# One step of Strassen in the first MLP product: seven block products, weight sums on GpSimd, last norm block by block

## The chip, the core and the metric

The kernel runs on one core of one Trainium2 chip. The metric is the device time in microseconds (us) of one execution, as the median of several. Five engines work side by side: TensorE (PE in the profile, with its weight loads as PEld), VectorE (DVE), ScalarE (ACT), GpSimd (POOL) and SyncE (SP), which issues the transfers. They wait for one another through semaphores.

## What is computed

A network of two blocks over 1024 tokens of width 1024 (an attention and convolution block of two layers, then a mixer block), and at its end an MLP and a norm. The change touches only this end:

```python
h = rms_norm(x, norm_mlp)                      # 1024 tokens x 1024
u = jnp.square(jax.nn.relu(h @ w_up))          # 1024 x 4096
x = x + u @ w_down                             # back to 1024 x 1024
return rms_norm(x, norm_final)
```

All is float32. The kernel keeps that accuracy on a bfloat16 array: each operand is split into a high part (rounded to bfloat16) and a low part (the rest), and each product is three matmuls (`mm3`: high x high, low x high, high x low).

## The kernel before

**Weights.** All weights come as 130 chunks of 128 x 2048 float32 (1 MB), in one order, `CHUNKS`. SyncE loads chunk n into one of two places of `stage` once chunk n-2 has been split. GpSimd (the loop from L504) splits it: four casts of 128x512 to `w_hi` (L513), four subtractions of 128x512 to `w_lo` (L520). `w_hi` and `w_lo` hold four chunks, so the split of chunk n waits until TensorE has used chunk n-4.

**MLP.** The 4096 hidden channels are taken in 16 rounds of 256. Chunk `up{j}` is the 1024 x 256 piece of the up weights of round j, `dn{j}` the 256 x 1024 piece of the down weights. TensorE's order is `MLP`: up0, up1, dn0, up2, dn1, ... up15, dn14, dn15. An up chunk is 96 matmuls of 128x512 (`gemm_f`: two groups n of 128 channels, two halves of the tokens, eight steps of k, three matmuls each). A down chunk is 96 too (eight token tiles t, 12 matmuls for each half). `ht_hi`, `ht_lo` (hT) hold the normed input, transposed: 128 x 8 x 1024.

**After an up chunk.** For each n: ScalarE evacuates PSUM with relu into RT[n] (`evac`, L1361), VectorE squares RT[n] (`squared`, L2104), ScalarE casts it into the high part of RS (L1477), VectorE subtracts for the low part (`square_lo`, L2108). RS holds two rounds. After a down tile VectorE adds it into the residual XR (`add_down`, L2116). VectorE's order is by hand: in round j the square of up j+1 comes ahead of the eight adds of dn j.

**PSUM.** There are eight banks of 128x512 float32: `big0`, `big1` (two banks each) and `bank[0..3]`. A tile of 1024 columns takes two. The pool "mlp" turns through four such tiles: big0, big1, banks 0 and 1, banks 2 and 3. `take` makes TensorE wait for whoever last read the banks it takes.

**Beginning of the MLP.** up0 runs inside `first_gemm(3, ...)` (L604) while the last parts of hT are written by `ht_half`; its two results lie in big1 (n = 0) and big0 (n = 1). up1 takes big0 first, so it waits for the evacuation of up0, n = 1.

**End.** ScalarE computes the sum of squares of each token tile as soon as its last add is done (L1484, L1486). SyncE loads the gain NF after the last matmul, and then VectorE makes the eight output tiles (L2139 reciprocal, L2142 multiply), through two buffers FO that go out by transfers of 512 KB (L494).

## Time and profile before

| | |
|---|---|
| time, median of 3 runs (range) | 3247.94 us (3245.13 to 3251.59) |
| profiled execution: its time / its span | 3242.97 us / 3241.1 us |
| TensorE busy | 3021.7 us, 93% of the span |
| VectorE, ScalarE, GpSimd busy | 55%, 33%, 29% |
| mean granted TensorE clock | 0.967 of full |
| matmuls of the 16 MLP rounds | from about 2553 us to 3217.7 us of the span |

The profile is of one execution. Its page lists busy time by engine and by group of instructions (line, engine, operation, tiles, shapes). The trace behind it can be asked for stretches of time, for waits (which engine waited for which instruction), and for instructions in order of time. A matmul is shown with a duration of 0.38 us, but matmuls are pipelined: what counts is the distance from one start to the next.

### The profile page before, as it was taken

Reading aid. Unit: us, or ns where it says so; the run is one execution under the profiler, and the core shown is the slowest. Engines: PE = TensorE matmul, PEld = TensorE weight load, DVE = VectorE, ACT = ScalarE, POOL = GpSimd, SP = SyncE. Lnnn points to the kernel's source line nnn. Section 1 sums busy time; section 2 is a strip of 40 time slices with the busy share of each in tenths; the row PEclk is TensorE's granted clock in tenths of the full one; section 3 lists DMA queues with packets and bytes.
Section 4 is the critical chain, followed back from the end, with each engine's and each line's share of the span. In section 5 each row is a group of like instructions: output and inputs, shape, how many; then the busy total and the mean of one; then the engine's idle time right before and its main releaser. Section 6 shows DMA issues by size and latency. Waiting matters only on the chain.

```text
span 3241.1 us, 48311 instructions
## 1 busy us (share of the span) xinstructions
PE 3021.7 (93%) x19783; PEld 1875.1 (58%) x20010; DVE 1767.4 (55%) x2951; ACT 1070.0 (33%) x1880; POOL 948.3 (29%) x958
## 2 busy tenths in 40 slices
PE   7979997999979978989999999999999999999997
PEld 7439875884439658854555655655654444444443
DVE  2575796773589976645265364365363333333334
ACT  2353544662356636633122132222122211001111
POOL 2301364000603470004323223323221433333320
PEclk9997998999999989999999999999899999999998
DMA  7313231002201321022111111111112111111101
GB/s 242 135 59 121 74 129 66 15 21 98 88 14 67 127 95 31 25 85 85 52 40 39 40 40 40 39 40 40 40 40 78 65 52 52 52 48 46 51 27 59
DMA packets 49164, 207.13 MB, mean 64 GB/s; under 512 B 4488, under 2 KB 9776, under 8 KB 32304
## 3 DMA queue, kind: packets, MB, share of 16 engines
q1 hardware_dynamic: 42288, 195.63, 17.2%
q10 hardware_dynamic: 6656, 8.39, 0.8%
q8 instruction: 159, 2.61, 0.3%
q14 instruction: 61, 0.50, 0.0%
HBM read 187.22 MB, written 16.79 MB: 63 GB/s over the span
## 4 chain that ended last, share of the span: by engine, by line
PE 79%; DVE 14%; issue 3%; ACT 3%; DMA 1%; POOL 1%; SPq 0%; DVEq 0%; ACTq 0%; POOLq 0%
PE big L268 18%; PE big L269 18%; PE big L267 18%; PE banks L267 4%; PE banks L268 4%; PE banks L269 4%; PE banks L1015 3%; DVE arena L1686 2%; PE banks L874 1%; DVE arena L1911 1%; PE big L550 1%; PE banks L550 1%; DVE arena L2075 1%; DVE arena L1891 1%; DVE arena L2020 1%
## 5 line engine op out<-in xcount | busy, mean ns | idle before, releaser
L513 POOL CAST w_hi<-stage 128x512 bf16<-128x512 f32 x432 | 282.2, 695 | 1796.4 <-PE big L269 1427.6
L520 POOL TENSOR_TENSOR w_lo<-stage,w_hi 128x512 bf16<-128x512 f32 x520 | 670.4, 1320 | 397.3 <-ACT w_hi L1187 396.6
L268 PE MATMUL big<-ht_lo,w_hi 128*128 128x512 bf16 x1412 | 536.7, 380 | 4.8 <-DVE ht_lo L1584 1.8
L267 PE MATMUL big<-ht_hi,w_hi 128*128 128x512 bf16 x1388 | 527.3, 380 | 13.0 <-DVE arena L1938 6.5
L269 PE MATMUL big<-ht_hi,w_lo 128*128 128x512 bf16 x1414 | 537.2, 380 | 1.5
L267 PE MATMUL big<-w_hi,ht_hi 128*128 128x256 bf16 (+1 forms) x1272 | 381.3, 300 | 18.1 <-POOL w_lo L520 9.2
L268 PE MATMUL big<-w_lo,ht_hi 128*128 128x256 bf16 (+1 forms) x1274 | 382.2, 300 | 4.0 <-issue 3.7
L269 PE MATMUL big<-w_hi,ht_lo 128*128 128x256 bf16 (+1 forms) x1276 | 382.3, 300 | 0.3
L267 PEld LDWEIGHTS big<-ht_hi,w_hi 128*128 128x128 bf16 x1440 | 143.1, 99 | 180.8 <-issue 14.9
L269 PEld LDWEIGHTS big<-ht_hi,w_lo 128*128 128x128 bf16 x1440 | 141.2, 98 | 171.0 <-issue 1.9
L268 PEld LDWEIGHTS big<-ht_lo,w_hi 128*128 128x128 bf16 x1440 | 141.3, 98 | 163.5 <-issue 4.4
L1361 ACT ACTIVATE arena<-big 128x1024 f32<-128x1024 f32 x66 | 67.5, 1023 | 429.0 <-PE big L269 428.8
L1699 DVE TENSOR_SCALAR_CACHE_REDUCE arena<-arena,smalli 128x512 bf16<-128x512 f32 (+5 forms) x268 | 206.7, 827 | 2.4
L267 PEld LDWEIGHTS big<-w_hi,ht_hi 128*128 128x128 bf16 x1280 | 151.0, 118 | 62.3 <-issue 10.8
L267 PE MATMUL banks<-w_hi,arena 128*128 128x128 bf16 (+2 forms) x696 | 174.7, 273 | 8.3 <-POOL w_lo L520 6.3
L268 PE MATMUL banks<-w_lo,arena 128*128 128x128 bf16 (+2 forms) x700 | 176.2, 274 | 0.4
L269 PE MATMUL banks<-w_hi,arena 128*128 128x128 bf16 (+2 forms) x698 | 175.6, 274 | 0.2
L269 PEld LDWEIGHTS big<-w_hi,ht_lo 128*128 128x128 bf16 x1280 | 150.4, 117 | 39.2 <-issue 1.7
L1263 ACT ACTIVATE arena<-arena,smalli 128x896 bf16<-128x896 f32 x124 | 134.8, 1088 | 115.0 <-DVE smalli L1845 115.0
L268 PEld LDWEIGHTS big<-w_lo,ht_hi 128*128 128x128 bf16 x1280 | 150.3, 117 | 38.1 <-issue 1.1
L1015 PE MATMUL banks<-arena 128*128 128x64 f32 x896 | 120.9, 291 | 29.7 <-DVE arena L2029 23.4
L1015 PEld LDWEIGHTS banks<-arena 128*128 128x128 f32 x896 | 115.7, 207 | 55.5 <-DVE arena L2029 43.0
(325 smaller groups left out, 5947.1 us busy)
## 6 DMA issues: line engine op xcount, KB each, us to landing
stage<-in_w SPq DMA_DIRECT2D x130, 1024.0 KB, 4.8
arena<-in_w_ada SPq DMA_DIRECT2D x48, 512.0 KB, 4.2
arena<-in_x SPq DMA_DIRECT2D x16, 512.0 KB, 7.5
xs<-arena SPq DMA_DIRECT2D x16, 512.0 KB, 2.6
arena<-xs SPq DMA_DIRECT2D x16, 512.0 KB, 7.8
gt<-arena ACTq DMA_DIRECT2D x16, 256.0 KB, 2.5
arena<-gt ACTq DMA_DIRECT2D x16, 256.0 KB, 2.6
out_x<-arena SPq DMA_DIRECT2D x8, 512.0 KB, 2.6
```

The lines of the kernel that those rows point to most:

```text
L267: pe.matmul(out, ah, bh, start=start, stop=False)
L268: pe.matmul(out, ah, bl, start=False, stop=False)
L269: return pe.matmul(out, al, bh, start=False, stop=stop)
L513: pool.tensor_copy(w_hi[:, n % RING, c0:c1], stage[:, n % RAW_RING, c0:c1]).then_inc(s_w_hi_split, mark(s_w_hi_split, n, q))
L520: ins = pool.tensor_tensor(w_lo[:, n % RING, c0:c1], stage[:, n % RAW_RING, c0:c1], w_hi[:, n % RING, c0:c1], ALU.subtract)
L550: ins = pe.matmul(g[:, (n * 4 + q) * 8 + k:(n * 4 + q) * 8 + k + 1], ada_buf(i)[:, k % 2, q * P:(q + 1) * P], s_(S_C + k), start=True, sto ...
L874: ins = pe.transpose(g[:, (s - q0) * P:(s - q0 + 1) * P], PB[h % 2][:, s * P:(s + 1) * P], ident)
L1015: ins = pe.matmul(g[:, s * 64:(s + 1) * 64].rearrange("p (j h) -> p j h", h=h), KF[c][:, s * P:(s + 1) * P], q, start=True, stop=True)
L1263: ins = act.activation(is_over[tb], score[tb], ACT.Sign, scale=-1.0, bias=smalli[:, 8 + j:9 + j].bitcast(F32), accum_out=s_(S_CNT + j))
L1361: act.activation(out, tile(pool, *key)[:, :], func, **kw).then_inc(s_read_act, mark(s_read_act, *key))
L1686: dve.scalar_tensor_tensor(score[tb], PB[i % 2][:, 0:N], w, score[tb], ALU.mult, ALU.add).then_inc(s_acc, mark(s_acc, l, i))
L1699: ins = dve.tensor_scalar(is_over[tb], score[tb], thr(j), 0.0, op, ALU.add, accum_out=cnt[:, j:j + 1])
```

## The change

The pieces `up2` to `up15` (the constant `STRASSEN`) are computed by one step of Strassen's scheme, in Winograd's form. The weight piece is seen as 2 x 2 blocks of 512 x 128, hT as 2 x 2 blocks of 512 x 512. Seven products of such blocks take the place of eight; `seven_products` issues them, in the order p1, p2, p6, p5, p7, p3, p4, each into one bank of 128x512 of the new pool "st" (`bank[0..3]`, in turn, the turn going on from round to round).

- GpSimd makes, per up chunk, four sums of weight blocks (128x512, float32), then seven casts and seven subtractions for the parts of the seven weight operands, in place of four and four. The parts are laid in the chunk's place and in `SUMX`, which has two places. The first of these chunks, up2, waits until hT is complete.
- The four sums of hT blocks (`TT`, high and low parts) are made once, in two halves g, by VectorE and ScalarE together (`token_sums`): 14 operations of 128x1024 on VectorE and 4 on ScalarE for each half. The first half stands ahead of the evacuation of up0 on ScalarE and ahead of its square on VectorE, the second behind the last `square_lo` of up0.
- For a seven-product round ScalarE copies p1 from PSUM; VectorE joins the rest by seven additions of 128x512 with one input from PSUM (`quarters`), straight into RT. There is no relu on ScalarE: `squared` is now max with 0 and multiply in one instruction.
- At the end NF is loaded after the last up product (NF, FO and the ScalarE junk tile lie where `TT` was), and VectorE makes output tile t-1 right behind the add of tile t (`finish`).
- The host lays out the up weights of these rounds by block.

The core of the diff:

```diff
+STRASSEN = range(2, 16)
...
+        pools = {"big": two[0:2], "t": one[0:2], "o": one[2:4], "c": one[0:3], "f": one[3:4], "c2": two[2:4], "mlp": two, "st": one}
...
-            sp.wait_ge(s_gemm, when(s_gemm, "dn", 15, NT - 1))
+            sp.wait_ge(s_gemm, when(s_gemm, "st", 15, "p4"))
             sp.dma_start(NF, AP_["norm_final"].partition_broadcast(P)).then_inc(s_nf_in, mark(s_nf_in, by=16))
...
+                if CHUNKS[n][1].startswith("up") and int(CHUNKS[n][1][2:]) in STRASSEN:
+                    j = int(CHUNKS[n][1][2:])
+                    a11, a12, a22, a21 = [stage[:, n % RAW_RING, 512 * i:512 * (i + 1)] for i in range(4)]
+                    s1, s2, s3, s4 = SUMF
+                    if j == STRASSEN[0]:
+                        pool.wait_ge(s_ht_lo, when(s_ht_lo, "all", 3))
+                    else:
+                        pool.wait_ge(s_w_split, when(s_w_split, n - 2))
+                    pool.tensor_tensor(s1, a21, a22, ALU.add).then_inc(s_sum, mark(s_sum, j, 3))
+                    pool.tensor_tensor(s3, a11, a21, ALU.subtract).then_inc(s_sum, mark(s_sum, j, 5))
+                    pool.wait_ge(s_sum, when(s_sum, j, 3))
+                    pool.tensor_tensor(s2, s1, a11, ALU.subtract).then_inc(s_sum, mark(s_sum, j, 4))
+                    pool.wait_ge(s_sum, when(s_sum, j, 4))
+                    pool.tensor_tensor(s4, a12, s2, ALU.subtract).then_inc(s_sum, mark(s_sum, j, 6))
+                    parts = ((0, a11), (1, a12), (2, a22), (3, s1), (5, s3), (4, s2), (6, s4))
+                    for i, x in parts:
+                        if i > 2:
+                            pool.wait_ge(s_sum, when(s_sum, j, i))
+                        pool.tensor_copy(sum_part(j, i)[0], x).then_inc(s_sum_hi, mark(s_sum_hi, j, i))
+                    for i, x in parts:
+                        pool.wait_ge(s_sum_hi, when(s_sum_hi, j, i))
+                        hi, lo = sum_part(j, i)
+                        ins = pool.tensor_tensor(lo, x, hi, ALU.subtract)
+                    ins.then_inc(s_w_split, mark(s_w_split, n))
+                    continue
...
+            def seven_products(j):
+                b11, b21, b22 = [x[:, 0:4, 0:512] for x in hT], [x[:, 4:8, 0:512] for x in hT], [x[:, 4:8, 512:1024] for x in hT]
+                for name, i, b in (("p1", 0, b11), ("p2", 1, b21), ("p6", 4, TT[1]), ("p5", 3, TT[0]), ("p7", 5, TT[2]), ("p3", 6, b22), ("p4", 2, TT[3])):
+                    if j == STRASSEN[0] and name == "p6":
+                        pe.wait_ge(s_t_lo, when(s_t_lo, 1, 3))
+                    w = [x.rearrange("p (k n) -> p k n", k=4) for x in sum_part(j, i)]
+                    g = take(pe, "st", "st", j, name)
+                    for k in range(4):
+                        ins = mm3(pe, g, [x[:, k, :] for x in w], [x[:, k, :] for x in b], k == 0, k == 3)
+                    ins.then_inc(s_gemm, mark(s_gemm, "st", j, name))
+                chunk_used(2, f"up{j}", s_gemm)
             for c, j in MLP[1:]:
                 pe.wait_ge(s_w_split, when(s_w_split, CHUNK_AT[(2, f"{c}{j}")]))
-                if c == "up":
+                if c == "up" and j in STRASSEN:
+                    seven_products(j)
+                elif c == "up":
                     gemm_f(2, f"up{j}", 0, ("up", j, 0), pool="mlp")
                     gemm_f(2, f"up{j}", 1, ("up", j, 1), pool="mlp")
...
+            def token_sums(g):
+                for i in range(4):
+                    act.wait_ge(s_t_sum, when(s_t_sum, g, i))
+                    act.activation(TT[i][0][:, 2 * g:2 * g + 2, :], TS[(0, 1, 2, 0)[i]], ACT.Copy).then_inc(s_t_hi, mark(s_t_hi, g, i))
+            def square_hi(j, n):
+                if j >= 2:
+                    act.wait_ge(s_gemm, when(s_gemm, "dn", j - 2, NT - 1))
+                act.wait_ge(s_r2, when(s_r2, j, n))
+                act.activation(RS[j % 2][0][:, n, :], RT[n], ACT.Copy).then_inc(s_rs_hi, mark(s_rs_hi, j, n))
             for c, j in MLP:
-                if c == "up":
+                if c == "up" and j in STRASSEN:
+                    if j > STRASSEN[0]:
+                        act.wait_ge(s_c_out, when(s_c_out, j - 1, "u2"))
+                    act.wait_ge(s_gemm, when(s_gemm, "st", j, "p1"))
+                    act.activation(PU[0], tile("st", "st", j, "p1"), ACT.Copy).then_inc(s_p_out, mark(s_p_out, j))
+                    freed(s_p_out, "st", j, "p1")
+                    square_hi(j, 0)
+                    square_hi(j, 1)
+                elif c == "up":
+                    token_sums(j)
                     for n in range(2):
                         if j:
                             act.wait_ge(s_rs_lo, when(s_rs_lo, j - 1, n))
                         evac(RT[n], ACT.Relu, "up", j, n, pool="mlp" if j else "big")
-                        if j >= 2:
-                            act.wait_ge(s_gemm, when(s_gemm, "dn", j - 2, NT - 1))
-                        act.wait_ge(s_r2, when(s_r2, j, n))
-                        act.activation(RS[j % 2][0][:, n, :], RT[n], ACT.Copy).then_inc(s_rs_hi, mark(s_rs_hi, j, n))
+                        square_hi(j, n)
...
+            def token_sums(g):
+                near, far = slice(2 * g, 2 * g + 2), slice(4 + 2 * g, 6 + 2 * g)
+                b11, b12 = [[x[:, near, 512 * t:512 * (t + 1)] for x in hT] for t in range(2)]
+                b21, b22 = [[x[:, far, 512 * t:512 * (t + 1)] for x in hT] for t in range(2)]
+                def low(i):
+                    dve.wait_ge(s_t_hi, when(s_t_hi, g, i))
+                    dve.tensor_tensor(TT[i][1][:, near, :], TS[(0, 1, 2, 0)[i]], TT[i][0][:, near, :], ALU.subtract).then_inc(s_t_lo, mark(s_t_lo, g, i))
+                t1, t2, t3 = TS
+                step(dve.tensor_tensor(t1, b12[0], b11[0], ALU.subtract))
+                step(dve.tensor_tensor(t1, t1, b12[1], ALU.add))
+                dve.tensor_tensor(t1, t1, b11[1], ALU.subtract).then_inc(s_t_sum, mark(s_t_sum, g, 0))
+                dve.wait_ge(s_t_sum, when(s_t_sum, g, 0))
+                step(dve.tensor_tensor(t2, b22[0], t1, ALU.subtract))
+                dve.tensor_tensor(t2, t2, b22[1], ALU.add).then_inc(s_t_sum, mark(s_t_sum, g, 1))
+                step(dve.tensor_tensor(t3, b22[0], b12[0], ALU.subtract))
+                step(dve.tensor_tensor(t3, t3, b22[1], ALU.add))
+                dve.tensor_tensor(t3, t3, b12[1], ALU.subtract).then_inc(s_t_sum, mark(s_t_sum, g, 2))
+                low(0)
+                dve.wait_ge(s_t_lo, when(s_t_lo, g, 0))
+                dve.wait_ge(s_t_sum, when(s_t_sum, g, 1))
+                step(dve.tensor_tensor(t1, b21[0], t2, ALU.subtract))
+                dve.tensor_tensor(t1, t1, b21[1], ALU.add).then_inc(s_t_sum, mark(s_t_sum, g, 3))
+                low(1)
+                low(2)
+                low(3)
+                dve.wait_ge(s_t_lo, when(s_t_lo, g, 3))
+            def quarters(j):
+                def add(name, out, x, p, *after):
+                    dve.wait_ge(s_gemm, when(s_gemm, "st", j, p))
+                    for a in after:
+                        dve.wait_ge(s_c_out, when(s_c_out, j, a))
+                    dve.tensor_tensor(out, x, tile("st", "st", j, p), ALU.add).then_inc(s_c_out, mark(s_c_out, j, name))
+                c11, c12, c21, c22 = RT[0][:, 0:512], RT[0][:, 512:1024], RT[1][:, 0:512], RT[1][:, 512:1024]
+                dve.wait_ge(s_rs_lo, when(s_rs_lo, j - 1, 1))
+                dve.wait_ge(s_p_out, when(s_p_out, j))
+                add("c11", c11, PU[0], "p2")
+                freed(s_c_out, "st", j, "p2")
+                add("u2", PU[1], PU[0], "p6")
+                freed(s_c_out, "st", j, "p6")
+                add("t", c12, PU[1], "p5", "u2")
+                freed(s_c_out, "st", j, "p5")
+                add("u3", c21, PU[1], "p7")
+                add("c22", c22, c12, "p7", "t")
+                freed(s_c_out, "st", j, "p7")
+                add("c12", c12, c12, "p3", "c22")
+                freed(s_c_out, "st", j, "p3")
+                add("c21", c21, c21, "p4", "u3")
+                freed(s_c_out, "st", j, "p4")
             def squared(j, n):
-                dve.wait_ge(s_read_act, when(s_read_act, "up", j, n))
-                dve.tensor_tensor(RT[n], RT[n], RT[n], ALU.mult).then_inc(s_r2, mark(s_r2, j, n))
+                if j in STRASSEN:
+                    dve.wait_ge(s_c_out, when(s_c_out, j, "c21" if n else "c12"))
+                else:
+                    dve.wait_ge(s_read_act, when(s_read_act, "up", j, n))
+                dve.scalar_tensor_tensor(RT[n], RT[n], 0.0, RT[n], ALU.max, ALU.mult).then_inc(s_r2, mark(s_r2, j, n))
...
+            token_sums(0)
+            squared(0, 0)
+            square_lo(0, 0, 0, T)
+            squared(0, 1)
+            square_lo(0, 1, 0, T)
+            token_sums(1)
+            for j in range(16):
+                if j + 1 in STRASSEN:
+                    quarters(j + 1)
+                if j < 15:
+                    squared(j + 1, 0)
+                    square_lo(j + 1, 0, 0, T)
+                for t in range(NT):
+                    add_down(j, t)
+                    if j == 15 and t:
+                        finish(t - 1)
+                    if j < 15 and t == 0:
+                        squared(j + 1, 1)
+                    if j < 15 and t == 2:
+                        square_lo(j + 1, 1, 0, 512)
+                    if j < 15 and t == 3:
+                        square_lo(j + 1, 1, 512, T)
+            finish(NT - 1)
```

## Rows read from the trace of the kernel before

**Rows 1.** Stretch of the MLP rounds: length, busy (count) by engine, PEclk, DMA share, GB/s.

```profile
2600.00:3213.00 613.00, 610.00 (x2785) 277.88 (x2840) 230.40 (x198) 66.50 (x72) 192.13 (x211) 1.00 0.12 43
```

**Rows 2.** Waits of PE, 2566:2700: who waited for whom, us, times, longest.

```profile
PE big L267 <- ACT arena L1361: 1.2, 1, 1.2
```

**Rows 3.** VectorE in order of time (start, us, what, [idle, releaser]), two rounds' first squares.

```profile
2628.38 1.23 DVE L2104 TENSOR_TENSOR arena<-arena 128x1024 f32<-128x1024 f32 x1 [10.25 <-ACT arena L1361]
...
2669.82 1.22 DVE L2104 TENSOR_TENSOR arena<-arena 128x1024 f32<-128x1024 f32 x1 [10.26 <-ACT arena L1361]
```

**Rows 4.** Groups by shape, 2500:3241: count, busy us, mean ns, idle before.

```profile
L520 POOL TENSOR_TENSOR w_lo<-stage,w_hi 128x512 bf16<-128x512 f32 x128 | 159.6, 1277 | 0.0
...
L2116 DVE TENSOR_TENSOR arena<-arena,big 128x1024 f32<-128x1024 f32 x64 | 78.1, 1220 | 113.9 <-PE big L269 113.9
...
L2142 DVE SCALAR_TENSOR_TENSOR arena<-arena,small 128x1024 f32<-128x1024 f32 x8 | 10.3, 1285 | 4.4 <-DMA out_x<-arena 3.9 <-DVE small L2139 0.4
```

**Rows 5.** Line L1719: min/median/max ns, first and last start, shape.

```profile
L1719 DVE TENSOR_TENSOR arena<-banks,arena x16: 679/686/692, 347.6 to 1082.9; 128x512 bf16<-128x512 f32 x16
```

**Rows 6.** In order of time: a PSUM tile handed from PE to DVE and back.

```profile
2547.79 0.38 PE L269 MATMUL big<-w_hi,arena 128*128 128x512 bf16 x1
...
2548.20 1.22 DVE L2095 TENSOR_TENSOR arena<-arena,big 128x1024 f32<-128x1024 f32 x1 [8.28 <-PE big L269]
...
2549.68 0.38 PE L267 MATMUL big<-ht_hi,w_hi 128*128 128x512 bf16 x1 [1.52 <-DVE arena L2095]
```

**Rows 7.** In order of time: DVE, ACT and PE around the end of up0.

```profile
2563.67 2.76 DVE L1540 SCALAR_TENSOR_TENSOR ht_lo<-banks,small,ht_hi 128x512 bf16<-128x512 f32 x4 [4.11 <-ACT ht_hi L1079]
...
2571.23 1.06 ACT L1477 ACTIVATE arena<-arena 128x1024 bf16<-128x1024 f32 x1 [1.29 <-DVE arena L2104]
2574.09 1.02 ACT L1361 ACTIVATE arena<-big 128x1024 f32<-128x1024 f32 x1 [1.81 <-PE big L269]
...
2575.26 0.38 PE L267 MATMUL big<-ht_hi,w_hi 128*128 128x512 bf16 x1 [1.21 <-ACT arena L1361]
```

**Rows 8.** The chain that ended last: start us, us, two dependent VectorE steps.

```profile
2471.00 1.24 DVE arena L2083
2472.27 1.24 DVE arena L2084
```

**Rows 9.** POOL in order of time: a split alone, then one beside VectorE.

```profile
2561.48 2.28 POOL L513 CAST w_hi<-stage 128x512 bf16<-128x512 f32 x4
2563.72 4.49 POOL L520 TENSOR_TENSOR w_lo<-stage,w_hi 128x512 bf16<-128x512 f32 x4
2574.19 3.27 POOL L513 CAST w_hi<-stage 128x512 bf16<-128x512 f32 x4 [5.98 <-PE big L269]
...
146.21 7.43 POOL L520 TENSOR_TENSOR w_lo<-stage,w_hi 128x512 bf16<-128x512 f32 x4
```

**Rows 10.** VectorE in order of time, beside the last two rows of Rows 9.

```profile
2575.15 1.28 DVE L2104 TENSOR_TENSOR arena<-arena 128x1024 f32<-128x1024 f32 x1 [1.61 <-ACT arena L1361]
...
147.25 4.27 DVE L1647 TENSOR_TENSOR arena<-arena 128x1024 bf16<-128x1024 f32 x2
```

**Rows 11.** PE in order of time after an idle stretch, then a window as in Rows 1.

```profile
234.39 0.43 PE L267 MATMUL big<-w_hi,ht_hi 128*128 128x256 bf16 x1 [4.66 <-DVE arena L1517]
...
238.88 0.32 PE L267 MATMUL big<-w_hi,ht_hi 128*128 128x256 bf16 x1
...
236.00:238.00 2.00, 2.00 (x11) 1.56 (x10) 2.00 (x5) 0.00 (x0) 0.00 (x0) 0.50 0.00 0
```

**Rows 12.** In order of time: the last add, the last sum of squares, output, last multiply.

```profile
3217.78 1.22 DVE L2116 TENSOR_TENSOR arena<-arena,big 128x1024 f32<-128x1024 f32 x1 [1.37 <-PE big L269]
...
3220.22 0.29 ACT L1486 ACTIVATE small<-small 128x1 f32<-128x1 f32 x1
...
3223.64 14.25 SPq L494 DMA_DIRECT2D out_x<-arena  x8
...
3236.25 1.28 DVE L2142 SCALAR_TENSOR_TENSOR arena<-arena,small 128x1024 f32<-128x1024 f32 x1 [0.38 <-DVE small L2139]
```

More of the change, by code:

```diff
@@ L1483, in _ @@
                     act.wait_ge(s_sq, when(s_sq, "m", 3, NT - 1))
[L1484 removed]
+                act.activation(JNK_END, XR[:, i, :], ACT.Square, accum_out=s_(S_SSQ + i)).then_inc(s_sq, mark(s_sq, "f", 4, i))
                 act.wait_ge(s_sq, when(s_sq, "f", 4, i))
@@ L2110, in square_lo, with finish @@
                     ins.then_inc(s_rs_lo, mark(s_rs_lo, j, n))
[L2112 to L2135 removed]
+            def finish(i):
                 dve.wait_ge(s_rms, when(s_rms, "f", 4, i))
@@ L2214, in pack_2 @@
     for j in range(16):
-        put(2, f"up{j}", f["w_up_2"][0][:, j * 256:(j + 1) * 256])
+        up = f["w_up_2"][0][:, j * 256:(j + 1) * 256]
+        if j in STRASSEN:
+            for i, (n, k) in enumerate(((0, 0), (0, 1), (1, 1), (1, 0))):
+                part = up[k * 512:(k + 1) * 512, n * P:(n + 1) * P].reshape(4, P, P).transpose(1, 0, 2)
+                w[CHUNK_AT[(2, f"up{j}")]][:, i * 512:(i + 1) * 512] = part.reshape(P, 512)
+        else:
+            put(2, f"up{j}", up)
         put(2, f"dn{j}", f["w_down_2"][0][j * 256:(j + 1) * 256, :])
```

51 lines of the change are left out of this document (23 added, 28 removed).

## The prediction

> **What bounds the kernel now.** I first read the windows by engine, for the stretch in which the MLP rounds run undisturbed. The reader is to see TensorE busy 610.0 of 613.0 us at a granted clock of 1.00, GpSimd busy 192 us, VectorE 230 us [rows 1]. Then the waits of TensorE: between 2566 and 2700 us of the span there is one, 1.2 us, and it lies ahead of up1 [rows 2]; asked for 2590 to 3213 us, the same view lists none. So these rounds are bound by the number of matmuls alone, and the other engines lie beside them. One round lasts from one first square to the next, 2669.82 - 2628.38 = 41.44 us [rows 3], for 192 matmuls: 0.2158 us each. Two places of the MLP are not bound so: its beginning, where ScalarE and VectorE stand between up0 and up1 [rows 7], and its end, where 23.4 us of the span come after the last matmul (it ends just before the last add starts, at 3217.78) [rows 12].
>
> **Fewer matmuls.** Seven products of 12 matmuls are 84 in place of 96. 14 rounds x 12 x 0.2158 = 36.3 us less on TensorE, all of it on the path. Weight loads stay one for each matmul. The round becomes 41.44 - 2.59 = 38.85 us.
>
> **GpSimd.** A cast costs 2.28/4 = 0.57 us, a subtraction of 128x512 4.49/4 = 1.12 us when nobody disturbs it [rows 9]; the four sums have two float32 inputs and a float32 output, which no row shows; the nearest is that subtraction, and I take 1.12 (between 0.57, the one-input row, and 1.86, the disturbed subtraction of rows 9). A pair of chunks costs 4 x 1.12 + 7 x 0.57 + 7 x 1.12 + (2.28 + 4.49) = 23.1 us of 38.85. The split of up j may begin when up j-2 is used and is needed two down chunks and one up chunk later, 59.6 us. It is hidden even if it doubles. The transfers of chunks wait for splits two back, and are hidden with them.
>
> **VectorE in a round.** The seven joins have one input from PSUM; the nearest row is 0.69 us for 128x512 [rows 5]. Per round: 8 adds x 1.22, 7 joins x 0.69, two squares now at 1.28 (the three-operand form) and two low parts at 1.23 [rows 3, 4]: 19.6 us of 38.85. The joins follow the products (2.59 us each) one by one and end with p4. What is new is the order: the first square now waits for the last product. Counted from the end of p4: join 0.8, square 1.3, ScalarE's cast 1.2, low part 1.3, first add 1.2: 5.8 us; with squares and low part slowed by GpSimd (below) 7.8. The fifth down tile, which takes the first one's banks, starts at 10.4. Hidden, with 2.6 us to spare.
>
> **The handover of p4's bank.** This is not hidden. The pool "st" goes on turning, so p4 lies in bank (6 - (j - 2)) mod 4: for j = 3, 4, 7, 8, 11, 12, 15 this is bank 0 or 1, which the first down tile takes. There TensorE must wait until VectorE has read p4. The same handover with an operation of 1.22 us put the next matmul 1.67 us behind its place (2547.79 + 0.22 to 2549.68) [rows 6], so 0.45 plus the operation: 0.69 + 0.45 = 1.14 us, 7 times: 8.0 us. In the other seven rounds p4 lies in bank 2 or 3, and the second down tile comes 2.59 us later: nothing. Bounds: 0 and 14 x 1.14 = 16.
>
> **Token sums at the beginning.** TensorE ends up0 just before 2574.09, and up1 can start when ScalarE has evacuated up0, n = 1: at 2575.26 now [rows 7]. In the changed order ScalarE does that after its cast of the first square, which comes after the first square, which comes after all 14 VectorE operations of the first token sums. These begin when hT is complete, 2563.67 + 2.76 = 2566.4. Dependent steps follow at 1.27 us [rows 8], independent ones at about 1.14: 17.4 us undisturbed. But GpSimd starts up2's sums at that very moment, since it waits for the same event. How the two slow one another: where GpSimd subtracts, two VectorE operations with two SBUF inputs took 4.27 us (clean 2.46), and GpSimd's four took 7.43 (clean 4.49) [rows 9, 10]: VectorE goes at 0.57 of its pace, GpSimd at about 0.44. Where GpSimd casts, VectorE took 1.28 for 1.23, and GpSimd lost 0.99 us beside it: 0.96 and 0.23. So: GpSimd's four sums last 4.49/0.44 = 10.2 us, in which VectorE does 5.8 of its 17.4 us; the other 11.6 run beside casts in 12.1. The sums end at 2588.7. Then square 1.3, cast 1.1, evacuation 1.0, handovers 0.3: up1 starts at about 2592.4, **17.1 us later** than now. TensorE has then idled 18 us, and its clock falls: after 4.66 us of idleness it ran at half (a granted 0.50) from 234.39 to 238.88 us [rows 11], which lost 2.2 us; I take 2.2.
>
> The second token sums come after the remaining squares and low parts of up0 (about 2598) and run beside GpSimd's subtractions of up2, then its casts and subtractions of dn1: by the same rates about 23.7 us, to 2621.6. The evacuation of up1, n = 1, whose banks the fourth tile of dn0 takes, waits behind them and a square, a cast and itself: 2626. The fourth tile could start at 2592.4 + 20.7 + 2.2 + 3 x 2.59 = 2623.1: 3.0 us lost. The beginning costs 17.1 + 2.2 + 3.0 = 22.3 us. If nothing slowed anything: sums to 2583.8, up1 at 2587.6, 12.3 + 2.2 = 14.5 us.
>
> The Trainium skill, GPSIMD Engine Reference, Key points, says that GpSimd's SBUF interfaces contend with VectorE instructions that have two SBUF inputs, and makes no exception for casts. The rows above show next to no slowing of VectorE beside casts, and I go by them; what the rule gives taken literally is rival 2 below.
>
> **The end.** Now: last matmul 3217.7, last add 3217.78 to 3219.0, last sum of squares and root to 3220.51, last multiply to 3237.53, span to 3241.1 [rows 12]. After: the gain is there, seven tiles are out already, and behind 3220.51 come 0.2 of reciprocal, one multiply of 1.28 [rows 4] and the same 3.6 us of output: 3225.6. **15.5 us less.** Within dn15 VectorE has an add, a reciprocal and a multiply per tile, about 2.55 us against TensorE's 2.59: just hidden, with four tiles of PSUM as a cushion.
>
> **Sum.** 36.3 + 15.5 - 8.0 - 22.3 = 21.5 us less. The profiled execution of before took 3242.97 us (span 3241.1): 3221.5 by it. The median of the runs shown is 5 us higher, 3247.94, and the same difference gives **3226.5**, my forecast for the median.
>
> **Rivals**, all against the median:
> 1. *The sums aren't slowed.* Reading bfloat16 or the four-byte sums could leave GpSimd's and VectorE's accesses apart. For: operations with a PSUM input keep 1.22 throughout [rows 4]. Against: rows 9 and 10. Beginning 14.5: 3218.7.
> 2. *Every one of the 28 token operations is slowed*, at 2.17 us, whatever GpSimd does. Then the first sums end at 2597.4, up1 starts at 2601.8 (26.5 late), the second sums end at about 2639 and dn0 waits 10.9, each with a clock loss of 2.2: 41.8 us. 36.3 + 15.5 - 8.0 - 41.8 = 2.0: 3246. Against: the row beside casts.
> 3. *GpSimd becomes the bound*, the case on the other side. Its pair of chunks adds time from 38.85 us on, and the kernel becomes slower than before by 0.2% where the pair passes 41.4 us (28 us lost, and the 8.0 of p4 hidden, over 14 rounds). With all 15 two-input operations at 7.43/4 = 1.86 us and half of the 11 casts stretched to 0.57/0.23 = 2.5 us a pair takes 27.9 + 13.7 + 3.1 = 44.7: 5.9 us a round over, x 14 = 83 us, while the waits for p4 (8.0) vanish in it: 3301. Against: it needs VectorE on two SBUF inputs almost all the time, and it is so for 5.0 us a round.
> 4. *Joins later than the products.* Every round waits at the first down tile, and for two joins, not one: 14 x (0.45 + 1.38) = 25.6 in place of 8.0: 3244. For: the joins are a chain with waits of VectorE on itself. Against: half its time is free.
> 5. *The products don't come at 0.2158 us a matmul*: seven groups of 12 with a look at a semaphore each in place of two of 48. Each group 0.1 us later is 9.8 us: 3236. The down tiles of before have one for every 24 matmuls, and [rows 1, 3] leave no room for a gap.
>
> **How the numbers follow.** Forecast case 0.60 (3219 to 3235, the spread of the slowing and of the p4 wait), rival 1 0.14, rival 2 0.09, rival 3 0.03, rival 4 0.06, rival 5 0.08. The range 3214 to 3241 holds the forecast case, rivals 1 and 5 and part of 4; it leaves out 2, 3 and the rest. A measurement of this kernel can tell 0.2%, 6.5 us, from no change: faster means under 3241.4. Faster: 0.60 + 0.14 + 0.08 + 0.02 + 0.02 (the early parts of 2 and 4) = 0.86; same 0.10; slower 0.04.
>
> **What would show it.** Matmuls 168 fewer, and rounds of about 38.9 and 40.0 us. In the waits of TensorE: seven waits of about 1 us on the last join, one of about 18 us on ScalarE's evacuation ahead of up1, and a few us in dn0. The clock at half for some us behind up1's start. Token operations of 1.2 to 2.2 us, by what GpSimd does. About 8 us between the last matmul and the end of the span. A wait of TensorE on w_lo in the rounds would show rival 3. The prediction is wrong if the beginning costs more than 40 us, or if each round waits.

## The result and the profile after

| | before | after |
|---|---|---|
| median (range, executions) | 3248.19 us (3245.13 to 3251.59, 4) | 3230.86 us (3228.2 to 3234.91, 4) |
| span of the profiled execution | 3241.1 us | 3226.4 us |
| first stretch: to hT complete | 2566.4 us | 2570.9 us |
| second stretch: from hT complete to the end | 674.7 us | 655.5 us |

The ratio after/before is 0.9947 (95% interval 0.9933 to 0.9961, so 13 to 22 us less): 17.3 us less by the medians, where 21.5 had been forecast. The last two rows cut each span where hT is complete, which is where the change begins to act (the last `ht_lo` operation on VectorE: 2563.67 + 2.76 before [rows 7], 2568.16 + 2.76 after). The first stretch holds the same instructions in both kernels. It came out between 2563.9 and 2573.3 us in the twelve profiles of this study, whatever the kernel, with the granted clock of TensorE in it 0.96 or 0.97. So single spans differ by up to 9 us for reasons outside the MLP, and below I compare second stretches: 19.2 us less.

The page's busy times after, then TensorE's waits from 2566 us to the end of the span (us in total, times, longest):

```profile
PE 2994.1 (93%) x19618; PEld 1864.1 (58%) x19842; DVE 1908.7 (59%) x3077; ACT 1058.3 (33%) x1874; POOL 1151.7 (36%) x1098
...
PE big L275 <- ACT arena L1418: 23.7, 2, 21.6
PE banks L275 <- DVE arena L2212: 6.4, 7, 1.0
```

Where before stood one wait of 1.2 us [rows 2] there are now nine: two on ScalarE's evacuation, seven on VectorE's last join (L2212 is the addition of `quarters`). The view shows nothing on the weight parts.

The beginning, in order of time (start us, us, engine and line); first VectorE with the token sums, GpSimd beside it, then ScalarE and TensorE, and windows as in [rows 1]:

```profile
2572.09 2.17 DVE L2188 TENSOR_TENSOR arena<-arena,ht_lo 128x1024 f32<-128x1024 f32 x1
...
2584.01 1.51 DVE L2195 TENSOR_TENSOR arena<-arena,ht_lo 128x1024 f32<-128x1024 f32 x1
...
2590.09 5.81 DVE L2184 TENSOR_TENSOR arena<-arena 128x1024 bf16<-128x1024 f32 x3
...
2595.94 2.06 DVE L2236 SCALAR_TENSOR_TENSOR arena<-arena 128x1024 f32<-128x1024 f32 x1
...
2573.14 2.25 POOL L536 TENSOR_TENSOR arena<-stage 128x512 f32<-128x512 f32 x1
...
2579.75 4.71 POOL L545 CAST w_hi<-stage 128x512 bf16<-128x512 f32 x3
...
2590.61 6.30 POOL L549 TENSOR_TENSOR w_lo<-stage,w_hi 128x512 bf16<-128x512 f32 x3
...
2598.99 1.01 ACT L1418 ACTIVATE arena<-big 128x1024 f32<-128x1024 f32 x1
...
2600.14 0.59 PE L275 MATMUL big<-ht_hi,w_hi 128*128 128x512 bf16 x1 [21.59 <-ACT arena L1418]
...
2602.00:2604.00 2.00, 2.00 (x7) 0.67 (x5) 1.29 (x1) 0.67 (x1) 2.00 (x2) 0.50 0.00 0
2604.00:2606.00 2.00, 2.00 (x7) 0.78 (x6) 1.58 (x2) 0.38 (x1) 2.00 (x3) 0.57 0.51 66
2606.00:2608.00 2.00, 2.00 (x11) 0.89 (x10) 1.97 (x2) 0.00 (x0) 2.00 (x3) 1.00 0.90 377
```

A token operation took 2.17 us beside GpSimd's two-input operations and 1.51 beside its casts; a cast beside it 4.71/3 = 1.57. The seven casts were done by about 2590.6, so the last three of the token operations met subtractions again: 5.81/3 = 1.94 us each. The first 14 ran from 2570.8 to 2595.9. TensorE idled 21.6 us, and its clock stood at half when it came back, until about 2605.7.

Two handovers of p4's bank, in TensorE's order of time, and the start of two up splits (GpSimd), one round apart:

```profile
2900.87 0.38 PE L277 MATMUL banks<-arena,w_lo 128*128 128x512 bf16 x1
2902.23 0.38 PE L275 MATMUL banks<-w_hi,arena 128*128 128x512 bf16 x1 [0.98 <-DVE arena L2212]
...
2743.81 1.26 POOL L535 TENSOR_TENSOR arena<-stage 128x512 f32<-128x512 f32 x1 [11.39 <-issue]
...
2783.80 1.27 POOL L535 TENSOR_TENSOR arena<-stage 128x512 f32<-128x512 f32 x1 [11.39 <-issue]
```

The next matmul comes 1.36 us after the last, not 0.22: 1.14 us lost. A round with a handover has 39.99 us, where 38.85 are the matmuls. GpSimd idles 11.4 us of it.

The end, to hold against [rows 12]: the last add, the last multiply, and the transfers of the output as SyncE issued them:

```profile
3219.03 1.22 DVE L2257 TENSOR_TENSOR arena<-arena,big 128x1024 f32<-128x1024 f32 x1
...
3221.99 1.28 DVE L2251 SCALAR_TENSOR_TENSOR arena<-arena,small 128x1024 f32<-128x1024 f32 x1
...
3206.13 17.51 SPq L511 DMA_DIRECT2D out_x<-arena  x8
```

From the start of the last add to the end of the span: 7.4 us, where it was 23.3.

### The profile page after: what moved, and what is told of

Same layout as the page of the kernel before. It is cut to its first block, busy times and chain, and to the rows that moved or that the text cites. A ratio compares the mean times of both kernels' runs of the same rounds, so it can differ in the third digit from the quotient of the medians.

```text
span 3226.4 us, 48326 instructions
## 1 busy us (share of the span) xinstructions
PE 2994.1 (93%) x19618; PEld 1864.1 (58%) x19842; DVE 1908.7 (59%) x3077; ACT 1058.3 (33%) x1874; POOL 1151.7 (36%) x1098
## 4 chain that ended last, share of the span: by engine, by line
PE 76%; DVE 16%; issue 3%; ACT 3%; POOL 1%; DMA 0%; SPq 0%; DVEq 0%; ACTq 0%; POOLq 0%
PE big L276 16%; PE big L277 16%; PE big L275 16%; PE banks L275 5%; PE banks L277 5%; PE banks L276 5%; PE banks L1057 4%; DVE arena L1760 2%; PE banks L916 2%; DVE arena L1985 1%; PE big L592 1%; PE banks L592 1%; DVE arena L2149 1%; DVE arena L1965 1%; DVE arena L2094 1%
## 5 line engine op out<-in xcount | busy, mean ns | idle before, releaser
L555 POOL CAST w_hi<-stage 128x512 bf16<-128x512 f32 x376 | 252.3, 713 | 1449.9 <-PE big L277 1241.1
L562 POOL TENSOR_TENSOR w_lo<-stage,w_hi 128x512 bf16<-128x512 f32 x464 | 600.6, 1326 | 396.8 <-ACT w_hi L1244 396.2
L275 PE MATMUL big<-ht_hi,w_hi 128*128 128x512 bf16 x1168 | 444.9, 381 | 33.4 <-ACT arena L1418 21.6
L276 PE MATMUL big<-ht_lo,w_hi 128*128 128x512 bf16 x1193 | 454.4, 381 | 4.5 <-DVE ht_lo L1658 1.8
L277 PE MATMUL big<-ht_hi,w_lo 128*128 128x512 bf16 x1194 | 454.4, 381 | 1.2
L275 PEld LDWEIGHTS big<-ht_hi,w_hi 128*128 128x128 bf16 x1216 | 121.2, 100 | 175.7 <-issue 36.1
L277 PEld LDWEIGHTS big<-ht_hi,w_lo 128*128 128x128 bf16 x1216 | 119.4, 98 | 145.1 <-issue 2.8
L276 PEld LDWEIGHTS big<-ht_lo,w_hi 128*128 128x128 bf16 x1216 | 119.3, 98 | 137.4 <-issue 4.9
L2212 DVE TENSOR_TENSOR arena<-arena,banks 128x512 f32<-128x512 f32 x98 | 66.2, 687 | 180.2 <-PE banks L277 180.2
L2094 DVE COPY_PREDICATED arena<-con,banks 128x512 f32<-128x512 int32 x56 | 58.8, 1049 | 164.7 <-PE banks L1057 164.5
L1057 PE MATMUL banks<-arena 128*128 128x64 f32 x896 | 124.7, 297 | 30.1 <-DVE arena L2103 23.7
```

The source lines that it names most:

```text
L275: pe.matmul(out, ah, bh, start=start, stop=False)
L276: pe.matmul(out, ah, bl, start=False, stop=False)
L277: return pe.matmul(out, al, bh, start=False, stop=stop)
L555: pool.tensor_copy(w_hi[:, n % RING, c0:c1], stage[:, n % RAW_RING, c0:c1]).then_inc(s_w_hi_split, mark(s_w_hi_split, n, q))
L562: ins = pool.tensor_tensor(w_lo[:, n % RING, c0:c1], stage[:, n % RAW_RING, c0:c1], w_hi[:, n % RING, c0:c1], ALU.subtract)
L1057: ins = pe.matmul(g[:, s * 64:(s + 1) * 64].rearrange("p (j h) -> p j h", h=h), KF[c][:, s * P:(s + 1) * P], q, start=True, stop=True)
```

## The experiments

My theory after this: the prediction's parts are right, and the beginning is dearer than forecast, since VectorE is slowed beside casts too. Rivals: the token operations are slow in themselves; the p4 waits are a symptom of something else; GpSimd paces the rounds after all. Second stretches of all kernels (hT complete to the end of the span, one profiled execution each), with the ratio of the executions' times to those of the kernel before. The intervals of after, e1_bank and e2_quiet overlap, so what those two edits are worth is read from the second stretch and the trace:

| kernel | second stretch, us | ratio (95% interval) | TensorE's waits in it, us |
|---|---|---|---|
| before | 674.7 | 1 | 1.2 |
| after | 655.5 | 0.9947 (0.9933 to 0.9961) | 23.7 evacuation, 6.4 joins |
| e1_bank | 652.0 | 0.9929 (0.9915 to 0.9944) | 26.5 evacuation |
| e2_quiet | 650.1 | 0.9937 (0.9925 to 0.9949) | 17.1 evacuation, 6.4 joins |
| e3_end | 659.3 | 0.9966 (0.9954 to 0.9978) | 1.2 |
| e4_order | 665.6 | 0.9973 (0.9962 to 0.9985) | 32.5 evacuation, 6.5 joins |
| e5_best | 626.9 | 0.9852 (0.9829 to 0.9875) | 2.9 evacuation |
| e6_sums2 | 662.6 | 0.9967 (0.9955 to 0.9978) | 29.2 evacuation, 6.4 joins |
| e7_parts2 | 668.0 | 0.9984 (0.9971 to 0.9996) | 25.8 evacuation, 6.5 joins, 6.7 adds |
| e8_same | 655.5 | one execution | 23.9 evacuation, 6.4 joins |
| e9_parts3 | 807.1 | one execution | 25.5 evacuation, 6.4 joins, 119.0 weight parts |
| e10_products | 673.9 | 0.9989 (0.9977 to 1.0) | 26.5 evacuation, 6.4 joins |

### e1_bank: the bank turn anew in every round

```diff
+                turns["st"] = 0
                 for name, i, b in (("p1", 0, b11), ("p2", 1, b21), ("p6", 4, TT[1]), ("p5", 3, TT[0]), ("p7", 5, TT[2]), ("p3", 6, b22), ("p4", 2, TT[3])):
```

> The changed kernel with one edit: the bank turn of the seven products starts anew in every round, so that the last product always lies in bank 2 and the first down tile never takes its bank. Theory (the seven waits of TensorE on the last join, 6.4 us by the view of waits plus the restarts, are what is left of the seven-product rounds' loss): 7 to 8 us less than the changed kernel, about 3223 us, no wait of TensorE on a join line, every seven-product round 38.85 us. Rival (the first down tile is late for another reason, such as VectorE's order, and the wait only moves to another releaser): the same time as the changed kernel, 3231 us, with as many waits on another line.

Its view of waits has no join, and its up splits start exactly 38.85 us apart (2747.75, 2786.60):

```profile
2747.75 1.27 POOL L535 TENSOR_TENSOR arena<-stage 128x512 f32<-128x512 f32 x1 [11.38 <-issue]
...
2786.60 1.27 POOL L535 TENSOR_TENSOR arena<-stage 128x512 f32<-128x512 f32 x1 [11.38 <-issue]
```

So the seven waits were the handover and nothing else. The total fell by less, 3.5 us of second stretch, because of the beginning: TensorE's restart in dn0 came 35.0 us behind up1's first matmul in place of 33.6 (1.4 us), and behind this longer wait, 4.9 us in place of 2.1, the clock stood at half for some 5.4 us, which cost another 2.7. The rest of the longer wait is time that TensorE had won just before: behind up1's start the clock was back at 2603.9, after 2.8 us, where it had taken 5.6. First TensorE's clock behind up1's start in e1_bank (the first matmul at 2601.06), its restart in dn0 and the clock there, then the same restart in the changed kernel:

```profile
2603.00:2604.00 1.00, 1.00 (x4) 0.36 (x3) 1.00 (x1) 0.00 (x0) 1.00 (x2) 0.57 0.00 0
...
2636.02 0.61 PE L275 MATMUL big<-w_hi,arena 128*128 128x512 bf16 x1 [4.94 <-ACT arena L1419]
...
2638.00:2642.00 4.00, 4.00 (x12) 1.49 (x11) 4.00 (x4) 1.06 (x1) 4.00 (x4) 0.57 0.00 0
```

```profile
2633.69 0.39 PE L275 MATMUL big<-w_hi,arena 128*128 128x512 bf16 x1 [2.15 <-ACT arena L1418]
...
2634.00:2638.00 4.00, 4.00 (x20) 1.78 (x19) 4.00 (x4) 0.91 (x1) 4.00 (x5) 1.00 0.00 0
```

In four microseconds 12 matmuls were recorded in place of 20. The edit doesn't touch this place. The profiles of the two differ in when GpSimd's split of up3 meets VectorE's second token sums (22.4 us behind up1's start in e1_bank, 23.8 in the changed kernel), so this term has a spread of its own: 4.9 us also in e10_products.

### e2_quiet: GpSimd waits for the first token sums

```diff
-                        pool.wait_ge(s_ht_lo, when(s_ht_lo, "all", 3))
+                        pool.wait_ge(s_t_lo, when(s_t_lo, 0, 3))
```

> The changed kernel with one edit: GpSimd starts the split of up2 only after the first token sums are done, not when hT is complete. Theory (the first token sums are slow because GpSimd works beside them): the first 14 VectorE operations take 17 to 18 us in place of 25, up1 starts 7 to 8 us earlier, the wait ahead of up1 falls from 21.6 to about 14 us; total 7 us less, about 3224 us. Rival (the token operations are slow in themselves, since they read bfloat16 and write float32): 25 us as before, and no change of the time, 3231 us.

The first token sums, VectorE in order of time, from 2569.85 to 2586.82:

```profile
2571.10 1.23 DVE L2188 TENSOR_TENSOR arena<-arena,ht_lo 128x1024 f32<-128x1024 f32 x1
...
2583.33 3.49 DVE L2184 TENSOR_TENSOR arena<-arena 128x1024 bf16<-128x1024 f32 x3
```

1.23 us for the operation that took 2.17, 17.0 us for the 14 that took 25.1. The operations aren't slow in themselves; what slows them is GpSimd. up1 began 20.3 us behind hT complete in place of 29.2. Of these 8.9 us 1.8 came back up to the restart in dn0, which came 35.4 us behind up1's first matmul in place of 33.6 (a wait of 4.4 in place of 2.1), because the up2 split now lay beside the second token sums. The clock, which had not fallen there in the changed kernel, stood at half for 3.4 us behind this restart: another 1.7. 5.4 us remain in the stretch.

### e3_end: the new end alone

```diff
-            sp.wait_ge(s_gemm, when(s_gemm, "dn", 15, NT - 1))
+            sp.wait_ge(s_gemm, when(s_gemm, "up", 15, 1))
...
                     add_down(j, t)
+                    if j == 15 and t:
+                        finish(t - 1)
```

(and NF, FO and ScalarE's junk tile at other addresses, as in the changed kernel).

> The kernel before with the new end alone: gain loaded after the last up product, output tile t-1 made behind the add of tile t, no block products. Theory (the end is worth what lies between the last matmul and the end of the span, 23.4 us before and 7.5 after): 15.9 us less than before, about 3232 us. Rival (part of that came from the earlier stages or is given back because the multiplies delay the adds): 3236 us or more, and waits of TensorE in the last down chunk.

15.4 us less in the stretch. From the start of the last add (3224.61) to the end of the span (3232.6) there are 8.0 us in place of 23.3, which is nearly all of it. The median is 3231.97 us, the ratio 0.9966: 11 us less, by its interval 7 to 15, so that the expected 15.9 lies just above. The executions alone would leave room for the rival, that part of the gain is given back; the trace shows no wait of TensorE in the last chunk, and nothing given back in the second stretch.

### e4_order: the first token sums behind up0's squares

```diff
-            token_sums(0)
             squared(0, 0)
             square_lo(0, 0, 0, T)
             squared(0, 1)
             square_lo(0, 1, 0, T)
+            token_sums(0)
             token_sums(1)
```

(and on ScalarE `token_sums(0)` behind the evacuation of up0).

> The changed kernel with the first token sums moved behind up0's evacuation, squares and low parts, on VectorE and ScalarE, nothing else. Theory (28 token operations stand on VectorE ahead of the first square of up1, and dn0 cannot go past its third tile without it, wherever in between they stand): no wait ahead of up1, but one of 18 to 24 us in dn0; total within 3 us of the changed kernel, 3228 to 3234 us. Rival (only the place ahead of up0's evacuation costs, the second half is hidden): 20 us less or more, 3210 us.

TensorE's restarts in dn0:

```profile
2627.19 0.61 PE L275 MATMUL big<-w_hi,arena 128*128 128x512 bf16 x1 [27.57 <-ACT arena L1418]
2635.01 0.61 PE L275 MATMUL big<-w_hi,arena 128*128 128x512 bf16 x1 [3.72 <-ACT arena L1418]
```

The wait left up1 (1.2 us there, as before the change) and came back whole in dn0, longer than I expected: 27.6 and 3.7 us. The total missed too: the stretch is 10.1 us longer than the changed kernel's, where I had put it within 3, and the median is 3236.12 us. The last restart came 70.3 us behind hT complete in place of 62.8, and the clock, at half behind both waits, cost 2.5 more. The 28 operations took 53.1 us here and 48.7 there. It is not the place ahead of the evacuation that costs but the queue: 28 slow operations on VectorE ahead of the first square of up1.

### e5_best: half the token sums behind dn0, products from up3 on

```diff
-STRASSEN = range(2, 16)
+STRASSEN = range(3, 16)
...
-            token_sums(0)
             squared(0, 0)
             square_lo(0, 0, 0, T)
             squared(0, 1)
             square_lo(0, 1, 0, T)
-            token_sums(1)
+            token_sums(0)
...
                     if j < 15 and t == 3:
                         square_lo(j + 1, 1, 512, T)
+                if j == 0:
+                    token_sums(1)
```

(and on ScalarE accordingly, with the bank turn of e1_bank).

> The changed kernel with seven-product rounds from up3 on (13, not 14), the bank turn anew in every round, the first token sums behind up0's squares and the second behind the adds of dn0. Theory (the beginning costs because 28 token operations stand ahead of the first square of up1; here only 14 do, and the other 14 stand beside up2 with nobody waiting): no wait ahead of up1, at most 3 us of waits in dn0 and dn1, none on a join. 13 x 2.59 = 33.6, plus 15.9 of the end, minus 2: 47 to 48 us less than before, a ratio of 0.985. Rival (as after moving the first sums alone, the wait comes back in dn0 at full length): 25 us less than before, 0.992.

The waits of TensorE from 2566 us on, all of them:

```profile
PE big L275 <- ACT arena L1419: 2.9, 2, 1.7
```

47.8 us less in the stretch, 0.9852 by the ratio: 3197.26 us, faster than both. One product round given up (2.6 us) buys a whole round in which 14 of the token operations have nobody waiting. The edit changes the first product round, both places of the sums and the bank turn at once, and no run shows their shares apart. The first token sums also took less, 21.7 us, because GpSimd idled 11.4 us beside them: up2 is an ordinary chunk here.

### e6_sums2, e7_parts2, e9_parts3: more work for GpSimd

Each makes part of GpSimd's work of a seven-product round again, in place: the four sums twice; the seven casts and subtractions twice; the same three times. The edit of e7_parts2:

```diff
                             pool.wait_ge(s_sum, when(s_sum, j, i))
+                        pool.tensor_copy(sum_part(j, i)[0], x).then_inc(s_sum_hi, mark(s_sum_hi, "again", j, i))
+                    for i, x in parts:
+                        pool.wait_ge(s_sum_hi, when(s_sum_hi, "again", j, i))
+                        hi, lo = sum_part(j, i)
+                        pool.tensor_tensor(lo, x, hi, ALU.subtract).then_inc(s_sum_hi, mark(s_sum_hi, "low", j, i))
+                    pool.wait_ge(s_sum_hi, when(s_sum_hi, "low", j, 6))
...
```

> The changed kernel with GpSimd's four sums made twice in each seven-product round (about 6 us more GpSimd work per pair of chunks, 27.4 to about 33.5 of 38.9 us). Theory (GpSimd is hidden in the rounds): rounds as long as in the changed kernel, no wait of TensorE on the weight parts; only the beginning, where VectorE and GpSimd work beside one another, grows by 2 to 6 us. Rival (GpSimd already sets the pace, or slows VectorE so far that TensorE waits): 6 us a round, 80 us more.

> The changed kernel with the seven casts and seven subtractions made twice in each seven-product round: about 14 us more GpSimd work, 41 to 43 us a pair of chunks against 38.9. Theory (GpSimd becomes the bound where its pair passes the round): every round as long as GpSimd's pair, 2 to 4 us more, waits of TensorE on the weight parts, the waits for the last join gone: 25 to 60 us more than the changed kernel. Rival (a lead of up to three chunks lets GpSimd be slower for 14 rounds without a wait): no more than 10 us.

> The changed kernel with the seven casts and seven subtractions made three times in each seven-product round. With them twice, GpSimd's pair of chunks took 39.0 us without a pause and TensorE never waited on the weight parts; three times is about 11.7 us more, 50.7 us. Theory (GpSimd is hidden until its pair passes the round of 38.85 to 40.0 us and then sets it one for one): rounds of 50 to 51 us once the lead is used up, waits of TensorE on the weight parts of 10 to 12 us in 12 or 13 rounds, 130 to 155 us more than the changed kernel. Rival (other limits, such as VectorE slowed by GpSimd, come first): waits mainly on joins and adds, and another length of the round.

With the sums twice the waits in the rounds stayed as they were and the beginning grew (7.1 us of stretch, a little over the 2 to 6 expected). With the parts twice neither expectation held: 12.5 us more, not 25 to 60 and not under 10. GpSimd's up splits then started 38.98 us apart without a pause (2830.09, 2869.07), not 41 to 43: I had put the extra work at 14 us, and it was nearer 12. That is just under the mean of 38.85 and 39.99, so GpSimd ran at the edge; TensorE never waited on the weight parts, but 6.7 us on adds, in two waits. VectorE in the second product round shows why, with two of GpSimd's groups beside it and TensorE's restart:

```profile
2743.73 12.27 DVE L2245 SCALAR_TENSOR_TENSOR arena<-arena 128x1024 f32<-128x1024 f32 x1
...
2746.76 4.50 POOL L571 TENSOR_TENSOR w_lo<-stage,w_hi 128x512 bf16<-128x512 f32 x4
...
2755.00 2.13 POOL L540 TENSOR_TENSOR arena<-stage,arena 128x512 f32<-128x512 f32 x1
...
2759.95 0.61 PE L275 MATMUL banks<-w_hi,arena 128*128 128x512 bf16 x1 [5.36 <-DVE arena L2266]
```

A square of 1.22 us took 12.27, while GpSimd's instructions followed one another without a gap. It ended 1.08 us behind the next gap of GpSimd (2754.92), ahead of L540, where GpSimd waits for a result of its own. The adds behind the square were late, and TensorE waited 5.4 us and restarted with the clock at half. Five more squares of e7_parts2 took 4.5 to 7.5 us, each ending 1.08 us behind such a gap or behind the end of GpSimd's work; in the changed kernel, where GpSimd pauses 11.4 us a round, none took over 2.3. So the first price of a GpSimd without pauses is VectorE's, as the rival of e6_sums2 had it, only at more work than that run had.

Three times over, one profiled execution took 3380.34 us, a second stretch 151.6 us longer than the changed kernel's (130 to 155 expected); TensorE's waits and two starts of an up split:

```profile
PE banks L275 <- POOL arena L567: 119.0, 13, 10.3
...
PE banks L275 <- DVE arena L2230: 6.4, 7, 1.0
...
2958.84 1.27 POOL L535 TENSOR_TENSOR arena<-stage 128x512 f32<-128x512 f32 x1
3009.79 1.27 POOL L535 TENSOR_TENSOR arena<-stage 128x512 f32<-128x512 f32 x1
```

Rounds of 50.95 us, as long as GpSimd's pair, thirteen waits on the low weight parts, each followed by a clock at half. So TensorE waits for GpSimd's parts only where GpSimd's pair is longer than the round, and then GpSimd sets the pace; a GpSimd that fills the round costs through VectorE before that. The changed kernel, with 11.4 us of idleness a round, is well inside.

### e8_same: was the row of the prediction special by its operands?

```diff
-                step(dve.tensor_tensor(t3, t3, b22[1], ALU.add))
+                step(dve.tensor_tensor(t3, t3, t3, ALU.add))
```

> The changed kernel with one operation of the token sums reading the same tile twice (t3 + t3 in place of t3 + the low part of hT, so this sum is left out). The prediction rested on one row, a square of RT with itself beside casts, 1.28 us; in the changed kernel the token operations beside casts take 1.51 to 1.62. Theory (the row was short because both inputs are the same tile): the operation that now reads t3 twice takes about 1.3 us beside casts, its neighbours 1.5. Rival (the row was short because it was one operation alone, at a lucky phase of the cast): 1.5 us like its neighbours. No change of the time beyond 1 us.

VectorE beside casts, the edited operation and the next:

```profile
2580.83 1.51 DVE L2194 TENSOR_TENSOR arena<-arena 128x1024 f32<-128x1024 f32 x1
2582.38 1.51 DVE L2195 TENSOR_TENSOR arena<-arena,ht_lo 128x1024 f32<-128x1024 f32 x1
```

Reading one tile twice makes no difference, and the stretch is that of the changed kernel (this kernel leaves out one of the sums, so its output isn't the network's; its instructions are as many and as large). Nor is it that the square stood alone: a low part with 1.12 us of idleness ahead of it took 1.63. What was special is the place in the cast, as the rival says. The cast that ran when the square of [rows 10] started, one cast of the chain of the changed kernel, and the low part with its cast:

```profile
2574.74 0.61 POOL L513 CAST w_hi<-stage 128x512 bf16<-128x512 f32 x1
...
2582.85 1.60 POOL L545 CAST w_hi<-stage 128x512 bf16<-128x512 f32 x1
...
2632.70 0.60 POOL L545 CAST w_hi<-stage 128x512 bf16<-128x512 f32 x1
2632.76 1.63 DVE L2240 TENSOR_TENSOR arena<-arena 128x1024 bf16<-128x1024 f32 x1 [1.12 <-ACT arena L1534]
```

| VectorE, both inputs in SBUF, 128x1024 | of GpSimd's running instruction still to come, us | took, us | difference |
|---|---|---|---|
| square at 2575.15, before | 0.21 of a cast | 1.28 | 1.07 |
| token operation at 2584.01, after | 0.44 of a cast | 1.51 | 1.07 |
| low part at 2632.76, after | 0.55 of a cast | 1.63 | 1.08 |
| square at 2595.94, after | 0.98 of a subtraction | 2.06 | 1.08 |

So such an operation takes the rest of the running GpSimd instruction and 1.07 to 1.08 us more, whatever that instruction is. This holds for all 55 operations of this shape in the changed kernel's MLP that started with at least 0.15 us of a GpSimd instruction to come, and for 596 of 604 in the twelve profiles; of the other eight six are the long ones of e7_parts2, one took 2.9 us in e9_parts3 and one 1.22. A cast that starts while such an operation runs takes that one's rest and 0.47 us more (1.13 and 0.47 in the chain: 1.60). In a chain each side therefore meets the other at the same place again, with 0.44 us to come; the square of [rows 10] met its cast when 0.21 was left. e5_best shows it again: a square beside casts, 1.28 us, at the same place in the cast.

### e10_products: the products alone, with the old end

```diff
-            sp.wait_ge(s_gemm, when(s_gemm, "st", 15, "p4"))
+            sp.wait_ge(s_gemm, when(s_gemm, "dn", 15, NT - 1))
...
-                    if j == 15 and t:
-                        finish(t - 1)
...
-            finish(NT - 1)
+            for i in range(NT):
+                finish(i)
```

> The changed kernel with the old end (gain loaded after the last matmul, output tiles made after all adds): the seven-product rounds alone. Theory (36.3 us fewer matmuls, of which the beginning gives back about 25 and the seven handovers 7.6, leaving 3 to 4 us): 1 to 5 us less than the kernel before, no change within 0.2%. Rival (the products gain more and the new end less): 10 us less than before or more.

0.8 us less in the stretch (with the longer second wait, 4.9 us), just under the 1 to 5 expected, and a ratio of 0.9989 with 1.0 at the edge of its interval. In the changed kernel, with the shorter wait, 3.3 of the 19.2 us are left when the end's 15.9 are taken off. The change's name-giving part is worth next to nothing as it stands; its gain is the end's.

## Why the prediction was right, and where it was off

The direction, the range and the parts held, with one part of the beginning mis-sized. In the changed kernel's second stretch:

| term | forecast, us | measured, us | from |
|---|---|---|---|
| fewer matmuls | -36.3 | -36.3 | rounds of 38.85 in e1_bank |
| end | -15.5 | -15.9 | 23.3 to 7.4 |
| p4 handovers | +8.0 | +7.6 | ten rounds, 395.0 us, hold six: 1.08 each |
| up1 later | +17.1 | +20.4 | 8.8 to 29.2 behind hT complete |
| clock behind it | +2.2 | +2.8 | half of 5.6 us at half clock |
| wait in dn0 | +3.0 | +2.1 | view of waits |
| sum | -21.5 | -19.3 | stretch: -19.2 |

**Matmuls, end, handovers.** Each came from rows of before and was met within 0.4 us. The handover (0.45 + the operation) was met: 1.14 us at 2900.87 and in two more of the seven, 1.03 in the other four. That it happens in seven rounds of fourteen followed from counting banks, and e1_bank shows it as cause.

**The step that failed** is the price of "the other 11.6 run beside casts in 12.1". It rested on one row, a square of 1.28 us beside casts [rows 10], read as a rate: 0.96 of VectorE's pace and 0.23 of GpSimd's. That square had met its cast with 0.21 us to come (e8_same). In the chain VectorE takes 1.51 for 1.23, 0.81, and GpSimd's cast 1.57 for 0.57, 0.36. So the operations beside casts were dearer, and, since the casts ended sooner, the last three of the sums didn't run beside casts at all but beside subtractions. Held against e2_quiet, the first five operations lost 3.8 us (4.4 forecast), the six beside casts 2.0 and the last three 2.3 (0.5 forecast for these nine). The sums took 25.1 us, not 22.3, and the square behind them, beside two-input work, 2.06, not 1.3: 3.5 us in all, of which the table has 3.3. The second sums, where both errors work against one another (GpSimd's casts end sooner, so that part of the sums runs free at 1.22), took 23.6 against 23.7.

**Luck.** That this came out so near is partly luck: the wait in dn0 was 2.1 us in the changed kernel and 4.9 in e10_products, whose beginning is the same code, and the clock behind up1's start cost 2.8 us here and 1.4 in e1_bank, behind the same idle 21.6 us. The forecast had one value for each.

**Mis-sized without effect.** A pair of chunks costs GpSimd 38.85 - 11.38 = 27.5 us, not 23.1: a sum alone takes 1.26, not 1.12, and some of its instructions meet VectorE in every round (2.25 for 1.26, in each round's second sum). VectorE was busy 21.7 us of the round from 2743.81, not 19.6. Both stay hidden.

The page of the Trainium skill named in the prediction, GPSIMD Engine Reference, Key points, speaks of contention with two-input VectorE instructions without an exception for casts; I had gone by the row against it. The rows of after side with the page in kind (1.51 beside casts is a slowing), while in size casts do much less than two-input work (2.17). Rival 2, the rule at full price throughout, would have given 41.8 us for the beginning; it was 25.3.

**Rivals.** 1 (no slowing) is refuted by e2_quiet, 3 (GpSimd as the bound) by the idle 11.4 us and by e9_parts3, which shows the point from which it would decide; 4 and 5 by the rounds of exactly 38.85 us in e1_bank.

**The rest,** 17.3 by the medians against 19.2 in the stretch, is within what the first stretch, up to the MLP, varies by from profile to profile. It was not traced further.

## What to carry to other kernels

Work moved off a full engine lands in somebody's queue: ask not only whether the other engine has time on average, but which small instruction of the next round stands behind the new work in its fixed order; here 28 one-time operations gave back two thirds of what 168 matmuls saved, and placing them otherwise won it back. When a buffer turn no longer divides evenly into the round, write down which buffer each round ends in, and who takes it next. How long an instruction takes beside another engine's depends on how much of the other is still to come when it starts; one row shows one such place and is not the rate of a chain. And leave the side engine pauses: where GpSimd had none, a square of VectorE took ten times its length.

## What the runs showed of the hardware

- Two VectorE and GpSimd instructions side by side, all in SBUF: VectorE 1.23 us (128x1024 float32) becomes 1.84 to 2.29 beside GpSimd's two-input operations (128x512, 1.12 to 1.27 alone, about 2.1 to 2.25 beside VectorE) and 1.51 to 1.63 beside its casts (0.57 alone, 1.57 beside). An operation of VectorE with one input in PSUM stayed at 1.21 to 1.22 and 0.69 throughout.
- In all these cases VectorE took the rest of the GpSimd instruction that ran at its start plus 1.07 to 1.08 us, and a cast that started beside VectorE the rest of that operation plus 0.47 (e8_same, 596 of 604 operations of this shape).
- Seven times, all where GpSimd's instructions followed one another without a gap (e7_parts2, e9_parts3), VectorE did not get its turn behind the running instruction but only at GpSimd's next gap: 12.27 us at the longest. Most of VectorE's operations there did get it; what decides was not traced.
- Idle stretches of TensorE of 3.7 (e4_order), 4.9 and 21.6 us were followed by a granted clock of 0.50, one of 2.15 us was not. It lasted 2.8 us (e1_bank) and 5.6 us (the changed kernel) behind the same 21.6.
